# Filter spectra from three products of rounded halves in place of fp32 products, with the dots' buffers loaded later

## The reference, cut to what matters

```python
h = sin(f1 * (z @ w1 + b1)); h = sin(f2 * (h @ w2 + b2))
h = (h @ w3).reshape(L, 2, 2, 512) * (decay + 0.05)[:, None, None, :]
taps = concat([(hf[0] + hb[0])[None], hf[1:], 0, hb[1:][::-1]])
spec = rfft(taps, axis=0)          # and row 0 takes the bias of the order
```

## Time and profile before

| what | value |
|---|---|
| median of 3 runs | 1113.68 us (1112.47 to 1114.11) |
| the profiled execution's own time | 1115.09 us |
| its span, first to last instruction | 1113.6 us |
| TensorE busy | 1091.2 us, 98% |
| VectorE busy | 801.9 us, 72% |
| ScalarE / GpSimd busy | 454.6 us, 41% / 109.2 us, 10% |
| mean granted TensorE clock | 0.995 |

### The profile page before, as it was taken

One profiled execution on the slowest core, in us unless ns is written; L12 is line 12 of the kernel. 1 busy time (PEld: TensorE's weight loads), 2 busy tenths in 40 slices (PEclk: granted clock), 3 DMA queues, 4 the chain that ended last, 5 costly groups with the idle time before them and its releaser, 6 DMA issues.

```text
span 1113.6 us, 16637 instructions
## 1 busy us (share of the span) xinstructions
PE 1091.2 (98%) x6304; PEld 1021.9 (92%) x6304; DVE 801.9 (72%) x1334; ACT 454.6 (41%) x792; POOL 109.2 (10%) x132
## 2 busy tenths in 40 slices
PE   6999999999999999999999999999999999999997
PEld 4787698888899999999899999999999999999886
DVE  5877699889388685556455777787978778788534
ACT  5721156665722322423346232253442526157424
POOL 2101210000334332000000000000000000000000
PEclk9999999999999999999999999999999999999998
DMA  9933454443332333743312331143333232222203
GB/s 347 378 100 116 153 189 135 133 132 112 113 131 105 119 104 124 280 148 111 114 57 94 119 127 57 57 152 97 113 100 109 95 104 95 87 76 76 95 19 115
DMA packets 45525, 138.85 MB, mean 125 GB/s; under 512 B 5051, under 2 KB 10635, under 8 KB 44556
## 3 DMA queue, kind: packets, MB, share of 16 engines
q1 hardware_dynamic: 29024, 80.21, 21.8%
q0 software_dynamic: 11376, 44.84, 11.5%
q10 hardware_dynamic: 5052, 12.81, 3.3%
HBM read 121.61 MB, written 15.74 MB: 123 GB/s over the span
## 4 chain that ended last, share of the span: by engine, by line
PE 91%; DVE 4%; DMA 1%; ACT 1%; issue 0%; DVEq 0%; ACTq 0%
PE acc_ps L750 39%; PE wk L1179 16%; PE acc_ps L1198 12%; PE acc_ps L832 12%; PE wk L1054 2%; PE acc_ps L839 1%; PE wk L989 1%; PE wk L978 1%; PE wk L968 1%; PE wk L1020 1%; PE wk L872 1%; PE wk L885 1%; DVE dot_out L1830 1%; PE wk L890 1%; DMA spec<-filt_out 1%; PE wk L880 0%
## 5 line engine op out<-in xcount | busy, mean ns | idle before, releaser
L750 PE MATMUL acc_ps<-act_hilo,w_hi 128*128 128x384 f32 x1504 | 332.2, 342 | 0.7 <-DVE act_hilo L1785 0.4
L750 PEld LDWEIGHTS acc_ps<-act_hilo,w_hi 128*128 128x128 f32 x1504 | 264.4, 188 | 19.5 <-issue 18.3
L750 PE MATMUL acc_ps<-act_hilo,w_lo 128*128 128x384 f32 x752 | 191.9, 336 | 0.0
L750 PEld LDWEIGHTS acc_ps<-act_hilo,w_lo 128*128 128x128 f32 x752 | 136.6, 188 | 0.0
L1198 PE MATMUL acc_ps<-hidden_hilo,act_hilo 128*128 128x384 f32 x768 | 134.7, 335 | 0.2
L1198 PEld LDWEIGHTS acc_ps<-hidden_hilo,act_hilo 128*128 128x128 f32 x768 | 133.2, 188 | 1.1 <-issue 1.0
L1739 DVE TENSOR_TENSOR w_lo<-w_raw,w_hi 128x1024 fp32r<-128x1024 f32 x61 | 76.3, 1251 | 54.9 <-ACT w_hi L1280 54.0
L1280 ACT ACTIVATE w_hi<-w_raw 128x1024 fp32r<-128x1024 f32 x61 | 64.2, 1052 | 44.3 <-PE acc_ps L750 40.9
L2195 DVE SCALAR_TENSOR_TENSOR xT<-acc_ps,modT,xT 128x512 f32<-128x512 f32 (+1 forms) x32 | 19.7, 617 | 59.8 <-PE acc_ps L832 59.6
L1830 DVE CUSTOM_DVE_ANT_0 dot_out<-dot_ring,c_rows,vecT 128x1024 f32<-128x1024 f32 x48 | 61.6, 1283 | 1.0
L2320 DVE SCALAR_TENSOR_TENSOR xT<-acc_ps,modT,xT 128x384 f32<-128x384 f32 (+2 forms) x96 | 40.5, 478 | 28.9 <-PE acc_ps L1198 28.9
(11 more groups left out here) (301 smaller groups left out, 2026.2 us busy)
## 6 DMA issues: line engine op xcount, KB each, us to landing
w_raw<-in_w_pre SPq DMA_DIRECT2D x50, 512.0 KB, 3.6
dot_ring<-in_w_ada_cols POOLq DMA_DIRECT2D x48, 512.0 KB, 3.8
w_raw<-in_w_up SPq DMA_DIRECT2D x32, 512.0 KB, 3.7
w_raw<-in_w_down SPq DMA_DIRECT2D x16, 512.0 KB, 3.5
w_raw<-in_w_down_half SPq DMA_DIRECT2D x32, 256.0 KB, 2.7
spec<-filt_out POOLq DMA_DIRECT2D x12, 512.0 KB, 3.1
gate_spill<-gates_out ACTq DMA_DIRECT2D x16, 384.0 KB, 2.3
hy_spec<-spec SPq DMA_DIRECT2D x12, 512.0 KB, 5.8
```

The costliest lines, as they stand in the source:

```text
L750: mm = pe.matmul(acc_ps[:, slot, 512 * h:512 * h + HALF], w[:, k, :], src[:, x, k, HALF * h:HALF * h + HALF], start=(first and i == 0), st ...
```

## The change

Spectrum units now run as three fp32r products each: table high by taps high, table high by taps low, table low by taps high. The tables come from the host already in halves (`filt_tab_hilo`, 128x2x1536, and `filt_tab_p_hilo`, 128x2x512). DVE writes a tap unit to one of two slots of `filt_tap`; ACT rounds it into `filt_taps_hi`; DVE subtracts into `filt_taps_lo` (`taps_low`). The low half of tap n is placed on DVE behind the multiply of tap n+1 of the same part, and the last one of a part at the head of the next spectrum unit. POOL's bias goes to the slot before ACT rounds it. A spectrum unit on PE waits for the low half of the one tap unit it reads (`tap_lo`), no longer for the whole part. The store waits on DVE are taken one result at a time.

For room, `filt_taps_lo` and `filt_tap` lie over `c_rows` and `dot_ring`, so `cb` and the first three dot loads are issued when unit f23 has been freed. The prompt decay is loaded into the place of the sample decay once f11 is freed, and the mask, whose place the tables take, is loaded by SP in its step t = 7 after f23 is freed; `softmax_in(0)` waits for it.

```diff
@@ sync
-            sp.dma_start(mask[:], a["t_mask"]).then_inc(ld_rope, 16)
...
+                if t == T_HY + 1:
+                    sp.wait_ge(f_free, len(FU))
+                    sp.dma_start(mask[:], a["t_mask"]).then_inc(ld_rope, 16)
@@ gpsimd
-            pool.dma_start(cb[:].rearrange("p g n -> p (g n)"), c_d.rearrange("r n -> (r n)").partition_broadcast(P)).then_inc(ld_c, 16)
...
-            for n in range(3):
-                dot_load(n)
...
+                if f + 1 == tap_end[0, 1]:
+                    pool.wait_ge(f_free, f + 1)
+                    pool.dma_start(dec[:, 0:2], a["t_decay_p"]).then_inc(ld_filt2, 16)
+            pool.wait_ge(f_free, len(FU))
+            pool.dma_start(cb[:].rearrange("p g n -> p (g n)"), c_d.rearrange("r n -> (r n)").partition_broadcast(P)).then_inc(ld_c, 16)
+            for n in range(DOTS_OUT):
                 dot_load(n)
@@ tensor, filt_unit
-                    pe.wait_ge(f_free, tap_end[g, r])
-                    pe.wait_ge(tap_bias, 2 * g + r + 1)
+                    pe.wait_ge(tap_lo, MODS + taps_for(f) + 1)
...
+                        for tab, m in terms:
+                            for x, y in ((0, taps_hi), (0, taps_lo), (1, taps_hi)):
+                                n += 1
+                                mm = pe.matmul(wk[:, c + at:c + at + 512], tab[x], y[:, p, m, :], start=(n == 1), stop=(n == 3 * len(terms)))
@@ scalar, filt_even
+                if kind == 0:
+                    n = taps_at.index(f)
+                    if (p, q) == (0, 0):
+                        act_e.wait_ge(tap_bias, 2 * g + r + 1)
+                    else:
+                        act_e.wait_ge(f_free, f + 1)
...
+                    act_e.activation(taps_hi[:, e, ms, :].rearrange("p m n -> p (m n)"), tap[:, n % 2], ACT.Copy).then_inc(tap_hi, 1)
+                    return
@@ vector
+            def taps_low(n):
+                lows[0] = n + 1
+                dve.wait_ge(tap_hi, MODS + n + 1)
+                e, ms = tap_slot(taps_at[n])
+                dve.tensor_tensor(taps_lo[:, e, ms, :].rearrange("p m n -> p (m n)"), tap[:, n % 2],
+                                  taps_hi[:, e, ms, :].rearrange("p m n -> p (m n)"), ALU.subtract).then_inc(tap_lo, 1)
@@ vector, filt_out
+                    if n >= 2:
+                        dve.wait_ge(tap_lo, MODS + n - 1)
+                    dve.tensor_tensor(tap[:, n % 2], wk[:, fu_col(f):fu_col(f) + 1024],
+                                      dec[:, 2 * q:2 * q + 2, :].rearrange("p m n -> p (m n)"), ALU.mult).then_inc(f_free, 1)
+                    if n % 4:
+                        taps_low(n - 1)
+                    return
+                while lows[0] < len([x for x in taps_at if x < f]):
+                    taps_low(lows[0])
```

More of the change, by code:

```diff
@@ L166, in program @@
             [("hidden_hilo", [P, 2, KD, T], F32R)])
-        (mraw_b,), (cb, ring, junk), (eo, eoT_hi, Y, yeo, yfull), (xT,) = region(
+        (mraw_b,), (taps_lo, tap), (cb, ring, junk), (eo, eoT_hi, Y, yeo, yfull), (xT,) = region(
             [("mod_raw_b", [P, 2 * MRING[1], 512], F32)],
+            [("filt_taps_lo", [P, 2, 4, 512], F32R), ("filt_tap", [P, 2, 1024], F32)],
             [("c_rows", [P, 2, D], F32), ("dot_ring", [P, 3, D], F32), ("dot_out", [P, D], F32)],
@@ L301, in program, with tap_slot, tap_reader, taps_for @@
                 spec_end[g, r] = len(FU)
+        taps_at = [f for f, unit in enumerate(FU) if unit[2] == 0]
+        def tap_slot(f):
+            g, r, _, e, mp = FU[f]
+            m0 = 2 * r if g else 2 * mp
+            return e, slice(m0, m0 + 2)
+        def tap_reader(f):
+            g, r, _, e, mp = FU[f]
+            if (g, r) == (0, 0):
+                return None
+            return FU.index((0, 0, 1, e, mp) if g == 0 else (0, 1, 1, e, r))
+        def taps_for(f):
+            g, r, _, p, q = FU[f]
+            return taps_at.index(FU.index((g, r, 0, p, q if g == 0 else 0)))
         fu_of = [0] * T_FILT + [6] * 4 + [0] * (T_MERGE - T_FILT - 4)
@@ L642, in _ @@
                     pool.wait_ge(f_free, f + 1)
-                    tap = taps[0:1, 0, 2 * r if g else 0, :]
-                    pool.tensor_tensor(tap, tap, pairs[0:1, 512 * r:512 * r + 512], ALU.add).then_inc(tap_bias, 1)
+                    first = tap[0:1, taps_at.index(f) % 2, 0:512]
+                    pool.tensor_tensor(first, first, pairs[0:1, 512 * r:512 * r + 512], ALU.add).then_inc(tap_bias, 1)
                 if kind == 1 and (g, kt) != (0, 0):
@@ L849, in filt_mlp, with even_tab, odd_tab, short_tab @@
                 mm.then_inc(fm_ready, 1)
+            def even_tab(p, j):
+                c = 256 * p + P * j
+                return [ftab[:, x, c:c + P] for x in range(2)]
+            def odd_tab(p, j, kt):
+                c = 512 + 512 * p + 256 * j + P * kt
+                return [ftab[:, x, c:c + P] for x in range(2)]
+            def short_tab(p, odd):
+                c = 256 * p + P * odd
+                return [ftab_p[:, x, c:c + P] for x in range(2)]
             def filt_unit(f):
@@ L1957, in filt_out @@
                     dve.wait_ge(n_hi, KD)
-                for x in range(e, specs[0]):
-                    if x >= 2:
-                        dve.wait_ge(f_stored[(x - 2) % 4], 16 * ((x - 2) // 4 + 1))
+                if g == 1:
+                    dve.wait_ge(f_stored[(e - 2) % 4], 16 * ((e - 2) // 4 + 1))
                 if g == 0:
@@ L2008, in softmax_in @@
                 b = n % 2
+                if n == 0:
+                    dve.wait_ge(ld_rope, 16 * 4)
                 if n >= 2:
@@ L2594, in tables @@
             out["t_filt_p"] = out["t_filt_p"][:, :, 0, :]
+    even = out["t_filt_s"][:, 0::2, :, 0:P].reshape(P, 512)
+    odd = out["t_filt_s"][:, 1::2].reshape(P, 1024)
+    for n, m in (("s", np.concatenate([even, odd], 1)), ("p", out["t_filt_p"].reshape(P, 512))):
+        m = m.astype(f)
+        bits = m.view(np.uint32)
+        high = ((bits + np.uint32(0x7FF) + ((bits >> np.uint32(12)) & np.uint32(1))) & np.uint32(0xFFFFF000)).view(f)
+        out[f"t_filt_{n}"] = np.stack([high, m - high], 1)
     return {k: np.ascontiguousarray(v.astype(f)) for k, v in out.items()}
```

72 lines of the change are left out of this document (33 added, 39 removed).

## The result

The changed kernel takes 1125.31 us (median of 5 runs, 1123.06 to 1127.1), the kernel before 1113.68 (1112.47 to 1114.11). The ratio is 1.0109, 95% interval 1.0092 to 1.0125: 12.1 us slower (the two medians differ by 11.6). The forecast was 1120.3 us with 1112.5 to 1124.0. The direction and the places were right; the size was about half of what came, and the median lies 1.3 us above the range.

What follows compares the result with a forecast made beforehand. TensorE, busy 1091.2 of 1113.6 us, was taken to bound the kernel. Work -5.2, waits 14.3 in place of 3.5 and store +1.0 made +6.6: 1121.7 us profiled, 1120.3 as the median, range 1112.5 to 1124.

Steps and rivals of the forecast that it cites:

- TensorE's work, -5.2: Spectrum units: 32 fp32 products become three fp32r matmuls each, 0.70 us in place of 0.86, 5.2 us less.
- The walk's waits: Filter units f0 to f23: TensorE's waits found by stepping through the engines' queues in code order, 11.4 us.
- The store, +1.0: f13's second store, beside a weight load: 2.6 us more if it takes 6.4, perhaps nothing; 1.0 taken.
- The dots, +2.9: Behind f23: `cb` and ring loads land late, VectorE idles 2.9 us before the first dot, TensorE waits as long.
- The clock, priced at nothing: TensorE's granted clock, from the filter units to the transposes: stays at 1.00, so no price is scaled.
- third rival: Slow store, late ring slots and one more meeting with POOL together, clock fall thinkable: beyond 1123.4 us; chance 0.11.
- The first: Filter stretch: VectorE's idle time takes in the added work, TensorE keeps its lead: 1106.8 to 1109.7 us; chance 0.10.

Runs made afterwards that it cites:

- experiment 7: experiment 1 with SyncE's weight load of tile 7 issued only once f13's two stores have landed: 1107.8 us, ratio 0.9943 to the kernel before.
- experiment 2: Kernel before with only `c_rows` and the first three dot buffers loaded behind f23: 1119.62 us, ratio 1.0052.
- experiment 3: Changed kernel without VectorE's 12 low-half subtractions, the high half read twice: 1118.73 us, ratio 1.0042 to the kernel before.
- experiment 8: experiment 6 with SyncE's weight load of tile 7 held until f13's two stores have landed: 1113.97 us, ratio 1.000 to the kernel before.
- experiment 13: experiment 8 with VectorE's rotary ops of tiles 4 and 5 one filter unit later: 1113.74 us, ratio 0.9993 to the kernel before.
- experiment 11: experiment 8 with `c_rows` issued only when the two stores ahead of it, of f20 and f21, have landed: 1115.82 us, ratio 1.0021 to the kernel before.
- experiment 6: Changed kernel with late tap roundings and one low half reordered, and buffers laid so the dots load before f23 is freed: 1116.78 us, ratio 1.0021 to before.
- experiment 1: Kernel before with three fp32r products per fp32 one, VectorE writing rounded taps, no tap split: 1111.36 us, ratio 0.9976.
- experiment 14: experiment 12 with SyncE's weight load of tile 10 issued only when the first dot buffer has landed: ratio 1.0053 to the kernel before.
- experiment 12: experiment 2 with both the four transform tables and the second and third dot buffers loaded later: ratio 1.0037 to the kernel before.
- experiment 4: Changed kernel with tiles laid out so the dots' buffers load before f23 is freed: 1120.68 us, ratio 1.0057 to the kernel before.
- experiment 9: experiment 2 with the four transform tables issued only when the third dot buffer has landed: ratio 1.0042 to the kernel before.
- experiment 10: experiment 2 with the second and third dot buffers issued only when `c_rows` and the first have landed: ratio 1.0069 to the kernel before.

## Why the prediction was right in kind and short in size

**TensorE's work, -5.2: right.** The chain has 1.39 and 1.40 us for a unit of two products (1.72 in the earlier trace rows). Alone and with the store out of the way the change gains 6.4 us (experiment 7). The rule of the Trainium skill (page FP8 and Floating Point Precision, TensorE Precision Notes: true fp32 in four passes) would have put it at 6.9. The 0.16 us for each product here don't bear that out.

**The walk's waits: right in place, too high in size.** Predicted and measured: f6 0.35 and 0.22, f9 0.84 and 0.64, f14 0.85 and 0.51, f15 2.84 and 2.46, f20 0.5 and 0.30, f21 3.8 and 3.44, f22 1.2 and none, the turn of v 1.1 and none; 11.4 in all and 7.6. What stands before f21 is as predicted. The timelines of VectorE and GpSimd:

```profile
125.54 1.23 DVE L1781 TENSOR_TENSOR w_lo<-w_raw,w_hi 128x1024 fp32r<-128x1024 f32 x1 [1.44 <-ACT w_hi L1310]
...
128.95 2.04 DVE L2058 TENSOR_TENSOR rope_rot<-rope_rot,rope_sin 128x768 f32<-128x768 f32 x1
...
132.84 1.22 DVE L1997 TENSOR_TENSOR filt_tap<-wk,filt_decay 128x1024 f32<-128x1024 f32 x1
```

```profile
127.98 2.20 POOL L662 TENSOR_TENSOR filt_tap<-filt_tap,hy_pairs 1x512 f32<-1x512 f32 x1 [6.23 <-DVE filt_tap L1997]
```

VectorE idles for ACT's late `w_hi`, then the rotary op meets the bias (2.04 beside 2.20, against 0.95 and 1.28 in the earlier trace rows), and tap f19 is only done at 134.06, when f21 starts. The Trainium skill's rule for two-input VectorE ops beside GpSimd (SBUF — State Buffer, Who interferes with whom) agrees with this meeting.

**The store, +1.0: a little low.** It took 6.2 us again, and f17 waited 1.70 us, where the walk had nothing and 1.0 was charged.

**The dots, +2.9: mis-sized, the first step that failed.** The prediction let `cb` (`c_rows`) land in 5.1 us and the first dot start at E + 7.5, at the latest at E + 9. `c_rows` landed in 6.9 us in the changed kernel; the 5.1 of the earlier trace rows is a median over the three loads in the kernel. The first dot began at E + 9.1 (144.64 to 153.73), and VectorE was idle 4.39 us. The transposes follow the first dot by 16.7 us in both kernels, so the term was 4.5 and not 2.9.

**The clock, priced at nothing: the second.** The prediction had: "The granted clock is 1.00 over both stretches, so no price has to be scaled", and kept the fall for the third rival. In the changed kernel it costs 1.4 us in f21 (2.83 against 1.40) and 0.4 in the k-step behind it, both on the chain: 1.8 us. Some of this stands where f22's wait of 1.2 had been forecast. VectorE freed f20 at 137.6, and at full clock TensorE would have come to f22 at some 136.6 and waited (an estimate from these rows):

```profile
136.93 0.68 DVE L2036 TENSOR_TENSOR filt_out<-filt_even,wk 128x512 f32<-128x512 f32 x1
```

The fall behind the wait of 2.41 us for `w_lo` (12 matmuls in 3.65 us, 2.1 at full speed) costs nothing of its own, since the transposes start 16.7 us behind the first dot with it and without it. In experiment 2 the clock fell behind the transposes, where nothing hid it, and there it cost 1.6.

**The sum again, from the rows.** It is taken in two pieces, up to E (the moment at which f23 is freed) and from E to the transposes.

| us | before | after | more | forecast |
|---|---|---|---|---|
| f0 to E | 66.60 to 141.64 | 64.07 to 144.64 | 5.5 | 3.7 (work -5.2, waits 10.3 for 2.4, store 1.0) |
| E to the transposes | to 162.94 | to 170.43 | 4.5 | 2.9 |
| behind them | | | 0.5 | nothing |

The first piece: waits 9.3 for 2.0, so +7.3 where the forecast had +8.9; work -5.2; clock +1.8; together 3.9. Most of the other 1.6 lies in how a wait is read. The idle time that a row shows is less than what the wait costs from start to start: ahead of f15 a k-step of 1.06 takes 3.69 us (107.83 to 111.52), 2.63 more for an idle time of 2.46, and f15 itself takes 0.1 more. That is some 0.26 us for each wait, and there are five more of them. The forecast had nothing for this. That the waits were put too high made up for about as much, and this is luck.

The profiled executions differ by only 8.0 us, since f0 started 2.5 us earlier in the one after; over all runs here it started between 64.07 and 66.60 us, in no relation to the change. The medians differ by 11.6, so 1.1 us more is in the timed executions. The profiled one is the fastest of the five, and the slower they are the lower is their granted clock (0.994 at 1123.06 us, 0.989 at 1127.1). So part of the 1.1 is probably clock again; no profile shows it. Of the 5.0 us between the forecast of +6.6 and the 11.6, 1.8 are thus in the first piece, 1.6 in the dots, 0.5 behind the transposes and 1.1 in these executions.

Apart, in kernels of their own: products -2.7, late dots +5.8, which leaves 9.0 of the 12.1 for the splits, and 7.5 went with the low halves (experiment 3).

**The rivals.** The first, that VectorE's idle time takes the work in, did not hold for the changed kernel. Its idle time was there in sum, and the reordered kernels show how much it can take in: with the same work in another order 12 us less, a tie with before (experiments 8 and 13), not the 1106.8 to 1109.7 of the rival. The third rival, with late ring slots and the clock, had two of the right mechanisms and too small a chance.

## What to carry to other kernels

Replacing TensorE passes by splits on the vector engines pays only as far as those engines stay ahead of it at each hand-over: here 5.2 us of saved matmul time bought 10 us of waits, and the order of three engines' queues decided over some 10 of the 12 us lost. Look for the slower matmuls behind a wait on TensorE: 1.5 to 1.8 us for a fall in these rows where TensorE's own work came next on the chain, nothing where it had to wait for VectorE again anyway. When TensorE gets faster, look at which fixed lateness (a store beside a load) it now runs into; one wait on the load's side gave back 3.7 us.

## What the runs showed of the hardware that I had not expected

- **The clock behind waits of TensorE.** The length of the wait alone does not tell whether it falls. It stayed at 1.00 behind waits of 1.5 to 1.9 us (before, experiments 8 and 11) and 2.2 us (experiment 6), and fell to 0.85 and 0.73 behind 3.2 us (experiment 1), and to 0.57 behind 2.8 (experiment 13) and 3.44 (after). But in experiment 14 it fell behind the wait of f17, which is 1.75 us, and the 12 matmuls behind f17 took 3.6 us where they take 2.1 in experiment 12. Its rows, the wait and then the window behind it:

```profile
119.44 0.50 PE L877 MATMUL wk<-filt_w_hi,filt_h_hilo 128*128 128x512 f32 x1 [1.75 <-DVE filt_out L1972]
```

```profile
120.00:124.00 4.00, 4.00 (x15) 3.88 (x14) 2.87 (x3) 0.00 (x0) 1.48 (x2) 0.57 0.54 217
```

  Near 2.5 us too it went either way: behind the same wait of f15 the windows of 112 to 116 us have 1.00 in the changed kernel and 0.67 in experiment 4. In experiment 2 it fell behind the second of two waits, 1.85 and 2.48 us, with 3.4 us of matmuls between them.
- **A store beside a weight load.** A store of 512 KB takes 3 us alone, and 5.0 to 7.1 as the second of a pair when a weight load of 512 KB on the other queue is issued within 0.6 us of it: 6.4 in the kernel before, where the load goes out ahead of it, and 6.2 in the changed one, where it goes out behind. In experiment 1 the pair and the load, 1.5 MB, need 8.4 us from the first issue to the last landing (106.94 to 115.3); in experiment 7 the pair alone, 1 MB, needs 4.3.
- **A queue of large loads.** Store, `c_rows` and one buffer behind one another, 2 MB, need 7.3 to 7.8 us from the second's issue in experiments 2, 9, 10, 12 and 14, whatever 2.5 MB of tables, buffers and weights do at that time. With the mask's load and other stores beside them it is more: 8.3 us in the changed kernel (145.46 to 153.73).
